# Twenty of forty modulation pairs move from the DeltaNet stage into the hybrid projection of a two-layer trunk

## What is computed

```
mod = split(silu(c) @ mod_w[layer] + mod_b[layer], 6)     # (1024) @ (1024 x 6144), for both layers
h   = rms_norm(x) * (1 + mod[1]) + mod[0]                 # mixer input, layer 0 (and hc for the context)
p   = h @ w_in ; pc = hc @ w_in[:, kv part]               # the hybrid projection
a   = gated DeltaNet in both directions (k, v, q, decay, beta from p and pc)
b   = grouped-query attention with QK norm and rotation (q, k, v from p and pc)
y   = concat(a, b) @ w_out
x   = x + mod[2] * rms_norm(y) ; h = rms_norm(x) * (1 + mod[4]) + mod[3] ; x = x + mod[5] * rms_norm(ffn(h))
layer 1: the same with a short-convolution mixer in place of the hybrid one
```

## Time and profile before

| | us |
|---|---|
| median of 3 runs | 1821.23 (1821.08 to 1822.94) |
| the profiled execution, whole | 1819.29 |
| its span, first to last instruction | 1817.4 |
| PE busy in it | 1718.3 (95%) |
| mean granted TensorE clock | 0.962 of full speed |

### The profile page before, as it was taken

How to read it: one execution, slowest core, us unless ns; L and a number is a source line. 1 busy time by engine, 2 the same in 40 slices (tenths; PEclk the granted TensorE clock), 3 DMA queues, 4 the chain that set the end, 5 groups by cost and what they waited for, 6 DMA issues and landing times.

```text
span 1817.4 us, 22614 instructions
## 1 busy us (share of the span) xinstructions
PE 1718.3 (95%) x9080; PEld 1429.1 (79%) x9080; DVE 982.6 (54%) x1242; ACT 704.5 (39%) x1058; POOL 323.4 (18%) x227
## 2 busy tenths in 40 slices
PE   8899997989988998989999999999999999999998
PEld 2788897889988955567788888887888688888886
DVE  2643277867697567757544444446446744444222
ACT  2432433344444478733433333223223244433321
POOL 3000014553464346512000000110002100000000
PEclk9899998999999968999999999999999999999999
DMA  8213041212221324032222332321322122332221
GB/s 337 68 54 81 16 151 47 71 47 70 93 70 48 117 70 139 24 93 83 80 93 93 105 100 84 104 94 52 108 96 93 47 93 92 104 103 87 87 87 64
DMA packets 153918, 161.14 MB, mean 89 GB/s; under 512 B 11383, under 2 KB 151144, under 8 KB 152680
## 3 DMA queue, kind: packets, MB, share of 16 engines
q1 hardware_dynamic: 153344, 159.74, 27.2%
q10 hardware_dynamic: 488, 0.18, 0.0%
HBM read 157.81 MB, written 2.10 MB: 88 GB/s over the span
## 4 chain that ended last, share of the span: by engine, by line
PE 82%; DVE 8%; ACT 4%; issue 2%; POOL 2%; DMA 0%; DVEq 0%; SPq 0%; ACTq 0%; POOLq 0%
PE ps L461 18%; PE ps L463 18%; PE ps L462 18%; PE ps L719 3%; PE ps L698 3%; PE ps L724 3%; ACT mod_raw_c L1107 2%; PE ps L509 1%; PE ps L810 1%; PE ps L827 1%; PE ps L829 1%; PE ps L828 1%; PE ps L784 1%; DVE w_lo L1389 1%; DVE dn_bl L1605 1%
## 5 line engine op out<-in xcount | busy, mean ns | idle before, releaser
L1389 DVE TENSOR_TENSOR w_lo<-w_raw,w_hi 128x2048 fp32r<-128x2048 f32 x100 | 229.1, 2292 | 512.7 <-ACT w_hi L1053 512.7
L461 PE MATMUL ps<-h_hi,w_hi 128*128 128x512 f32 x968 | 377.2, 390 | 0.4 <-DVE w_lo L1389 0.4
L462 PE MATMUL ps<-h_lo,w_hi 128*128 128x512 f32 x968 | 376.7, 389 | 0.0
L463 PE MATMUL ps<-h_hi,w_lo 128*128 128x512 f32 x968 | 376.7, 389 | 0.0
L1053 ACT ACTIVATE w_hi<-w_raw 128x2048 fp32r<-128x2048 f32 x100 | 191.2, 1913 | 320.9 <-PE ps L463 306.0
L1911 POOL TENSOR_TENSOR mod_raw_c<-mod_raw_c 128x1024 f32<-128x1024 f32 (+2 forms) x120 | 189.0, 1578 | 141.9 <-ACT mod_raw_c L1107 134.9
L461 PEld LDWEIGHTS ps<-h_hi,w_hi 128*128 128x128 f32 x968 | 181.7, 188 | 38.3 <-DVE w_lo L1389 0.8
L462 PEld LDWEIGHTS ps<-h_lo,w_hi 128*128 128x128 f32 x968 | 181.7, 188 | 37.6
L463 PEld LDWEIGHTS ps<-h_hi,w_lo 128*128 128x128 f32 x968 | 181.7, 188 | 37.7
L461 PE MATMUL ps<-mid_hi,w_hi 128*128 128x512 f32 x338 | 132.9, 393 | 0.0
L463 PE MATMUL ps<-mid_hi,w_lo 128*128 128x512 f32 x338 | 131.8, 390 | 0.0
(11 more groups left out here) (331 smaller groups left out, 2789.1 us busy)
## 6 DMA issues: line engine op xcount, KB each, us to landing
w_raw<-in_ffn_w_up SPq DMA_DIRECT2D x44, 1024.0 KB, 5.1
mod_raw_c<-in_mod_w SPq DMA_DIRECT2D x40, 1024.0 KB, 5.3
w_raw<-in_ffn_w_down SPq DMA_DIRECT2D x16, 896.0 KB, 4.6
w_raw<-in_sc_w_in SPq DMA_DIRECT2D x12, 1024.0 KB, 5.2
w_raw<-in_hyb_w_in SPq DMA_DIRECT2D x9, 1024.0 KB, 5.4
mod_raw_a<-in_mod_w SPq DMA_DIRECT2D x8, 1024.0 KB, 16.2
w_raw<-in_ffn_w_down SPq DMA_DIRECT2D x8, 1024.0 KB, 5.0
w_raw<-in_sc_w_out SPq DMA_DIRECT2D x4, 1024.0 KB, 5.0
```

Of the source, the lines that this page charges most:

```text
L461: mm(dst, hi, xh[:, k0 + k, :], start=first and k == 0, stop=False)
L462: mm(dst, hi, xl[:, k0 + k, :], start=False, stop=False)
L463: i = mm(dst, lo, xh[:, k0 + k, :], start=False, stop=last and k == nk - 1)
L1389: V.tensor_tensor(wlo[s][:, :], raw[s][:, :], f32(whi[s][:, :]), ALU.subtract).then_inc(sem("w_lo"), 1)
```

## The change

Pairs 0 to 19 leave the DeltaNet levels. They get two buffers of their own outside the ring: `mod_raw_e0` for the even pairs (the four `tmp` tiles) and `mod_raw_e1` for the odd ones (the place of the context input xc), and six buffers for finished sums (`mod_sums`). Projection unit u takes the pairs 2(u-1) and 2(u-1)+1 (`early_at`), from unit 1 to unit 10:

- SP loads the two pairs of stage u behind the raw weights of unit u+2, each when POOL has finished with the pair that had the buffer before (`mod_acc`).
- At the end of unit u's evacuation ACT multiplies the even pair (8 instructions) and DVE the odd one (one instruction of 128x2048).
- POOL adds pair after pair, and writes the last sum to one of the six sum buffers.
- PE makes the columns three units later, behind the unit's matmuls; those of the last four pairs come behind the item rows.
- DVE waits for the columns of all twenty ahead of `dn_ready`, since DeltaNet tiles lie over the new buffers.

Four pairs (20 to 23) stay in the levels, one in each of chunks 0 to 3: products at level 1, all three adds two levels later, columns four levels later. Pairs 24 to 39 stay where they were. The total of multiplications, adds and columns is the same, but for ten pairs the eight ACT instructions become one of DVE.

```diff
+        mraw_e = [view(place(f"mod_raw_e{i}", KC * UW, F32, a0), "p (k n) -> p k n", n=UW)
+                  for i, a0 in enumerate((tmp_at, R + 73 * K))]
+        macc = view(region("mod_sums", 6 * UW, 81), "p (j n) -> p j n", n=UW)
...
-        DN_PAIRS = 24
+        EARLY, LEVEL_PAIRS = 20, 4
...
+        def early_at(u):
+
+            return [j for j in range(EARLY) if j // 2 + 1 == u]
...
-        MOD_LEVEL = [LEVELS * (j // 4) + 2 * (j % 4) for j in range(DN_PAIRS)]
...
-            return [j for j, q0 in enumerate(MOD_LEVEL) if q0 + lag == q]
+            return [j for j in range(EARLY, EARLY + LEVEL_PAIRS) if LEVELS * (j - EARLY) + 1 + lag == q]
...
+            def load_early(j):
+
+                if j == 0:
+                    sp.wait_ge(sem("h"), 2 * KC)
+                elif j >= 2:
+                    sp.wait_ge(sem("mod_acc"), acc_c(j - 2))
+                sp.dma_start(mraw_e[j % 2][:, :, :], mod_source(j)).then_inc(sem(f"mod_e{j % 2}"), 16)
...
+                for j in early_at(u - 2):
+                    load_early(j)
...
             sp.dma_start(sinT[:, :], A["sin"]).then_inc(sem("rope_in"), 16)
-            for j in range(PAIRS):
+            for u in range(U_WOUT - 2, U_WOUT + 2):
+                for j in early_at(u):
+                    load_early(j)
+            for j in range(EARLY, PAIRS):
                 load_mod_pair(j)
...
+            def mod_columns(pairs):
+                for j in pairs:
+                    pe.wait_ge(sem("mod_acc"), acc_c(j))
+                    acc = macc[:, j % 6, :] if j < EARLY else mraw_c[(j - EARLY) % MSLOTS][:, 0, :]
+                    for part in range(2):
+                        mod_column(16 + 2 * j + part, acc[:, part * P:(part + 1) * P])
...
+                mod_columns(early_at(u - 3))
                 for e in ITEMS_IN.get(u - 1, ()):
                     item_stat(e)
...
+            for u in range(U_WOUT - 3, U_WOUT):
+                mod_columns(early_at(u))
...
+                early_products(u)
                 if u == 8:
 
                     dve.wait_ge(sem("abT"), 1)
...
+            dve.wait_ge(sem("mod_done"), 2 * EARLY)
             dve.wait_ge(sem("ge"), 3)
...
+            def mod_parts(j):
+
+                early = j < EARLY
+                slot = mraw_e[j % 2] if early else mraw_c[(j - EARLY) % MSLOTS]
+                pool.wait_ge(sem("mod_prod1" if early and j % 2 else "mod_prod"), j // 2 + 1 if early else j - EARLY // 2 + 1)
+                mod_add(3 * j, slot[:, 0:4, :], slot[:, 0:4, :], slot[:, 4:8, :])
+                mod_add(3 * j + 1, slot[:, 0:2, :], slot[:, 0:2, :], slot[:, 2:4, :])
+                if early and j >= 6:
+                    pool.wait_ge(sem("mod_done"), 2 * (j - 5))
+                mod_add(3 * j + 2, macc[:, j % 6, :] if early else slot[:, 0, :], slot[:, 0, :], slot[:, 1, :])
```

More of the change, by code:

```diff
@@ L638, in _ @@
                 item_rows(e)
-            def mod_columns(pairs):
-                for j in pairs:
-                    pe.wait_ge(sem("mod_acc"), acc_c(j))
-                    for part in range(2):
-                        mod_column(16 + 2 * j + part, mraw_c[j % MSLOTS][:, 0, part * P:(part + 1) * P])
+            for u in range(U_WOUT - 3, U_WOUT):
+                mod_columns(early_at(u))
             def gate_rows(s):
@@ L756, in _ @@
                     i.then_inc(sem("Sp"), 1)
-            for q in range(LEVELS * NT, LEVELS * NT + 5):
-                mod_columns(mod_at(q, 4))
             pe.wait_ge(sem("S"), 2 * NT)
@@ L1108, in products, with early_products @@
                 i.then_inc(sem("mod_prod"), 1)
+            def early_products(u):
+                for j in early_at(u):
+                    if j % 2 == 0:
+                        act.wait_ge(sem("mod_e0"), 16 * (j // 2 + 1))
+                        products(mraw_e[0])
             def square(e):
@@ L1170, in _ @@
             group_sd(2)
+            for u in range(U_WOUT, U_WOUT + 2):
+                early_products(u)
             act.wait_ge(sem("gcv"), 3)
@@ L1200, in _ @@
                     for j in mod_at(s * LEVELS + l, 0):
-                        act.wait_ge(sem(f"mod_in{j % MSLOTS}"), landed(j))
-                        products(mraw_c[j % MSLOTS])
+                        act.wait_ge(sem(f"mod_in{(j - EARLY) % MSLOTS}"), landed(j))
+                        products(mraw_c[(j - EARLY) % MSLOTS])
                 for d in range(2):
@@ L1450, in recip, with early_products @@
                 V.reciprocal(nsm[:, item_cols[g]], nsm[:, item_cols[g]]).then_inc(sem("nrc"), 1)
+            def early_products(u):
+                for j in early_at(u):
+                    if j % 2:
+                        dve.wait_ge(sem("mod_e1"), 16 * (j // 2 + 1))
+                        V.tensor_tensor(mraw_e[1][:, :, :], mraw_e[1][:, :, :], bc(cvec[:, :, 0], UW), ALU.mult).then_inc(sem("mod_prod1"), 1)
             dnw = lambda k, j: vec[:, 2, 12 * k + j:12 * k + j + 1]
@@ L1919, in _ @@
             pool.wait_ge(sem("h"), KC)
+            for j in range(EARLY):
+                mod_parts(j)
             pool.wait_ge(sem("rope_in"), 32)
-            def mod_parts(j, parts):
-                pool.wait_ge(sem("mod_prod"), j + 1)
-                for part in parts:
-                    mod_half(3 * j + part, mraw_c[j % MSLOTS])
-            def mod_level(q):
-                for lag, parts in ((3, (1, 2)), (2, (0,))):
-                    for j in mod_at(q, lag):
-                        mod_parts(j, parts)
             pool.wait_ge(sem("dn_ready"), 1)
@@ L1959, in _ @@
                         G.tensor_tensor(rope_tile(l - 1), rope_tile(l - 1), cosT[:, :], ALU.mult).then_inc(sem("rcos"), 1)
-                    mod_level(s * LEVELS + l)
-            for q in range(LEVELS * NT, LEVELS * NT + 4):
-                mod_level(q)
-            for j in range(DN_PAIRS, PAIRS):
-                mod_parts(j, (0, 1, 2))
+                    for j in mod_at(s * LEVELS + l, 2):
+                        mod_parts(j)
+            for j in range(EARLY + LEVEL_PAIRS, PAIRS):
+                mod_parts(j)
             for j in range(4):
```

19 lines of the change are left out of this document (9 added, 10 removed).

## The result

| | before | changed |
|---|---|---|
| median | 1822.09 (4 runs, 1821.08 to 1823.17) | **1863.55** (4 runs, 1845.46 to 1871.47) |
| profiled execution, whole | 1819.29 | 1871.47 |
| its mean clock | 0.962 | 0.940 |

A forecast was written before the change was run, and what follows sets the result against it. PE was taken to bound the kernel nearly everywhere. Costs of 43 to 63 us (projection 22 to 42, tail 21) against 40 gained, taken two thirds of the way, gave +16: median 1837, range 1820 to 1850.

The forecast's parts named there:

- What the DeltaNet stage gives back: DeltaNet chunks: moving the pairs out removes waits, late masks, columns and level 6 products, 40 us gained.
- the lower bound of 35: DeltaNet chunks: the gain is only 35 us if the four remaining pairs still catch a mask in each chunk.
- 8.1, 5.7 and 1.8: Chunk 0's losses: level 4, the stretch from there to the matmuls, and those matmuls being slow; together put at 15 us.
- The walk through the rounds: Projection: load, product and adds per buffer fall behind, delaying squares, abt and g; 22 us without port conflicts, 42 with.
- meetings: Projection: DVE and POOL block each other on shared SBUF ports, each meeting costing the loser up to 2.3 us.
- Behind the last unit: After the last projection unit: late loads and product 19 delay item rows, plus columns and lower clock, 21 us.
- The lower clock: PE rows after stands run slower: 3 us behind the last unit and 3 for the wait on g.
- the two-thirds step: Projection and tail cost 43 to 63 us; POOL busy two thirds of a stage, so two thirds of the way: +16.
- the first two terms: Cost up to g's matmuls, +35 (22 to 42), and from there to the gate rows, +21 us.
- the pairs keep pace: Projection: the loads' head start also covers squares, abt and g; 16 us faster, 1805; chance 0.13.
- no meetings occur: Projection: rounds of 13.3 us, PE waits for abt and g only, 43 against 40, 1824; chance 0.13.
- Every wait counts fully: Projection: all port conflicts occur and three PE waits each add 3 us of lower clock; 32 slower, 1853; chance 0.12.

The follow-up runs named there:

- three traces: Profiled runs of the unaltered changed kernel, one from each of three sets of runs: 1871.47, 1834.68 and 1843.61 us.
- the first trace: Profiled execution of the changed kernel's first set of four runs, nothing altered: 1871.47 us at mean clock 0.940.
- the two faster ones: Profiled runs of the two repeat sets of the changed kernel, nothing altered: 1834.68 us at clock 0.963 and 1843.61 us at 0.960.
- the kernel without early pairs: Changed kernel with the twenty early pairs' loads, products and additions left out, their columns taken from a constant tile: 1786.69 us, ratio 0.983.
- the second: Profiled run of the first repeat set (six runs) of the unaltered changed kernel: 1834.68 us, the fastest of that set.
- the fourteen runs: All runs of the unaltered changed kernel, in sets of four, six and four: 1834.68 to 1871.47 us, median 1848.8.

## Why the prediction was wrong in size and right in kind

**What the DeltaNet stage gives back: 40 predicted.** Measured 34.5 to 35.7 in three traces: the lower bound of 35. Chunk 0, from its gate rows to the next chunk's, took 59.1 us in the first trace where it took 69.5 before, so it gave 10 and not 15 (its parts, 8.1, 5.7 and 1.8, add up to 15.6).

**The walk through the rounds.** Right in order and place: abt at 229.7 (229 predicted for meetings), pair 13 summed at 222 (221), the square of item 3 reaching PE at 234.5 (235), unit 11 behind g at 260 (257). These times of the first trace came out within 3 us; in the two faster ones all of them lie 3 us or so earlier. But the end of the walk, 42, was in part luck. Less 5.5 for columns it holds 36.5 us of standing ahead of g's matmuls, 8 of it for item 0 (4.1 to 5.8 measured); the stands there were 23.8, 26.0 and 25.6 us in the three traces. Most of the difference was filled by the lower clock behind them, for which the walk had nothing: PE was busy up to g's matmuls for 6.3 to 9.8 us more than in the kernel without early pairs. The step that failed is the one behind the walk: "POOL is busy for about two thirds of a stage when DVE's instructions fall due, so I take two thirds of the way". Measured were 41 to 44, and I took 35. That both queues are late by then and seldom miss each other is argued; the traces show the lengths, 2992 ns for 2292 at the mean of ten splits.

**Behind the last unit.** 21 predicted, 17.5, 18.1 and 24.9 measured. The stand was 13.6 by the sum and 12.6 to 13.4 by the traces. The first trace has 7 more, with its item rows at 1.2 GHz for 15 us where I had allowed about 6.

**The lower clock.** I counted 3 us behind two stands, 6 in all. From 145 us to the gate rows PE was busy for 11.1, 12.0 and, in the first trace, 23.4 us more than in the kernel without early pairs (106.5). In the sum of the two faster traces that is hidden by the stands that I had too long.

**What was not in the sum at all** is that the stages behind might change. Attention was put at nothing because no instruction of it moved. It took 169, 149 and 155 us for 156. This is the largest piece of the miss in the first trace, where the sum was +16 and +52.3 was measured: attention 12.6 and what lies behind it 5.2, then 9.1 from the two-thirds step, 5.5 from the DeltaNet stage and 3.9 from the steps behind the last unit. With the first two terms put right, 42 + 18 - 35.5 = 24.5, the time is 1844 to 1846; with attention as in the first trace 18 more, as in the second 7 less. That is about the spread of the fourteen runs, and the first four had two of the three slowest. The 169 us stand in a trace of one of these three; the eleven others, at 1845.46, are where the corrected sum puts them. The range ended at 1850 because nothing in it allowed for that.

**The rivals.** That the pairs keep pace, and that no meetings occur, are both refuted. "Every wait counts fully", 1853, with its extra clock, was the nearest to the fourteen runs' 1848.8, and its chance of 0.12 was too small.

Left open: why attention's clock varies from run to run. In the three traces of kernels with the old DeltaNet stage attention took 154.6 to 156.1 us; in the fifteen of kernels with fewer pairs in the levels 148.0 to 168.7, so it may be shorter as well as longer. That fewer pairs are the cause is a guess from these traces.

## What to carry to other kernels

Work put into another engine's idle time is to be walked queue by queue: what counts is not how idle the engine is but what stands behind the new instruction in its program, and if two engines share a port and both are late, count every meeting that the rows allow, since the measured end lay there. A wait of the tensor engine in a stretch where it never waited costs its length and 3.5 to 4 us more here, and attention, with its varying clock, moved from 8 us shorter to 13 longer although nothing in it changed. Take several traces before a difference is explained. Move first what costs most where it is, and stop at the first pair that something waits for, here between the eighth and the tenth.

## What the hardware showed that I had not expected

- One kernel ran between 1834.7 and 1871.5 us, in step with its mean granted clock (0.963 to 0.940), while the kernel before stayed between 1818.5 and 1826.0 in all its runs but one of 3788.5.
- Four added stands of PE cost 46 us but left the runs 0.6 us apart.
- After one stand of 11.9 us the matmuls were at 1.2 GHz for some 7 us; after one of 13.4 us in the first trace of the changed kernel for 15, though PE was busy throughout (6.00 of 6.00 us from 294 to 300, clock 0.50). The Trainium skill, "TensorE: Matmul & The Clock Gate", section "Part 1: The HAM clock gate", has the clock fall when the engine idles, which the traces agree with (0.50 from 282 to 288, where PE did nothing); nothing measured here explains the 15 us.
- DVE's 128x2048 instruction and POOL's adds each lost about 2 us in one meeting (4.44 for 2.29, and 5.70 for 3.76).
